# State-space stage of a two-block model: decay rows repeated across partitions by DMA in place of products of ones

## What is computed

```python
xbc = silu(causal_conv4(xbc))            # xs: 16 heads of 64; bm, cm: 4 groups of 128 states
dt = softplus(dt_raw + dt_bias)
a_cum = cumsum(dt * -exp(a_log), within the chunk)
seg = a_cum[:, :, :, None] - a_cum[:, :, None, :]
lmat = exp(where(tril, seg, -inf))       # per head, 0 above the diagonal
cb = einsum('bclgn,bcsgn->bclsg', cm, bm)              # scores, per group
y_diag = einsum('bclsg,bclsgr,bcsgrp->bclgrp', cb, lmat, xdt)
states = einsum('bcsgn,bcsgr,bcsgrp->bcgrpn', bm, exp(a_cum[end] - a_cum), xdt)
y_off = einsum('bclgn,bcgrpn,bclgr->bclgrp', cm, carried_states, exp(a_cum))
g = (y_diag + y_off + d_skip * xs) * silu(z)
g = g * rsqrt(mean(g * g, over the 256 of a group) + eps) * norm_w
```

## Time and profile before

| | |
|---|---|
| median of 3 runs | 1828.46 us (1828.44 to 1828.81) |
| the profiled execution: its time / span of its instructions | 1829.15 us / 1827.4 us |
| mean granted TensorE clock | 0.991 |
| PE busy | 1764.4 us (97%) |
| PE weight loads busy | 1415.2 us (77%) |
| DVE busy | 1002.7 us (55%) |
| ACT busy | 574.9 us (31%) |
| POOL busy | 714.4 us (39%) |
| chain that ended last, by engine | PE 75%, DVE 20%, ACT 2% |

### The profile page before, as it was taken

One profiled execution on the slowest core, in us unless ns is written; L12 is line 12 of the kernel. 1 busy time (PEld: TensorE's weight loads), 2 busy tenths in 40 slices (PEclk: granted clock), 3 DMA queues, 4 the chain that ended last, 5 costly groups with the idle time before them and its releaser, 6 DMA issues.

```text
span 1827.4 us, 22151 instructions
## 1 busy us (share of the span) xinstructions
PE 1764.4 (97%) x7938; PEld 1415.2 (77%) x7938; DVE 1002.7 (55%) x1382; ACT 574.9 (31%) x796; POOL 714.4 (39%) x303
## 2 busy tenths in 40 slices
PE   7999999999999999999899999999989999999996
PEld 6877778788888887888778777777748777778885
DVE  4344333333322645113678989897599766576326
ACT  5322222322222224123632333333362323251211
POOL 3433333343444444443344324343314333325445
PEclk9999999999999999999899999999999999999998
DMA  5322222222333323332433222232212222217422
GB/s 200 114 81 81 81 82 92 81 81 81 99 103 92 97 95 131 116 126 69 163 93 114 69 70 93 62 88 81 69 36 92 81 69 69 80 58 252 126 83 92
DMA packets 50091, 175.55 MB, mean 96 GB/s; under 512 B 5217, under 2 KB 5473, under 8 KB 48865
## 3 DMA queue, kind: packets, MB, share of 16 engines
q1 hardware_dynamic: 41472, 152.13, 26.8%
q10 hardware_dynamic: 8544, 22.37, 3.4%
HBM read 166.09 MB, written 8.39 MB: 95 GB/s over the span
## 4 chain that ended last, share of the span: by engine, by line
PE 75%; DVE 20%; ACT 2%; issue 2%; POOL 1%; DMA 0%; ACTq 0%; DVEq 0%; SPq 0%; POOLq 0%
PE bank L330 73%; DVE gate L1065 3%; DVE feats L1053 2%; DVE bias L1053 2%; DVE bias L1553 1%; PE bank L334 1%; DVE top L1549 1%; DVE probs L1053 1%; DVE gT L1415 1%; DVE gate L1097 1%; DVE nmax L1092 1%; DVE tmp L1053 1%; DVE probs L1104 1%; DVE wide L1408 1%; POOL w_lo L308 1%
## 5 line engine op out<-in xcount | busy, mean ns | idle before, releaser
L308 POOL TENSOR_TENSOR w_lo<-raw,w_hi 128x1024 fp32r<-128x1024 f32 x280 | 688.8, 2464 | 1096.7 <-ACT w_hi L718 1096.7
L330 PE MATMUL bank<-planes_hi,w_hi 128*128 128x512 f32 (+1 forms) x1792 | 709.7, 396 | 19.0 <-DVE w_lo L1128 9.4
L330 PE MATMUL bank<-planes_lo,w_hi 128*128 128x512 f32 (+1 forms) x1792 | 694.8, 388 | 0.0
L330 PE MATMUL bank<-planes_hi,w_lo 128*128 128x512 f32 (+1 forms) x1776 | 687.7, 387 | 0.0
L718 ACT ACTIVATE w_hi<-raw 128x1024 fp32r<-128x1024 f32 x280 | 296.9, 1060 | 909.6 <-PE bank L330 893.3
L330 PEld LDWEIGHTS bank<-planes_hi,w_hi 128*128 128x128 f32 x1792 | 339.7, 190 | 110.2 <-issue 36.6
L330 PEld LDWEIGHTS bank<-planes_lo,w_hi 128*128 128x128 f32 x1792 | 340.1, 190 | 70.2 <-issue 4.8
L330 PEld LDWEIGHTS bank<-planes_hi,w_lo 128*128 128x128 f32 x1776 | 336.2, 189 | 68.3
L330 PE MATMUL bank<-w_hi,planes_hi 128*128 128x512 f32 x512 | 199.9, 391 | 4.2 <-DVE planes_lo L1069 4.2
L330 PE MATMUL bank<-w_hi,planes_lo 128*128 128x512 f32 x512 | 199.2, 389 | 0.0
L330 PE MATMUL bank<-w_lo,planes_hi 128*128 128x512 f32 x512 | 199.2, 389 | 0.0
(11 more groups left out here) (252 smaller groups left out, 1376.5 us busy)
## 6 DMA issues: line engine op xcount, KB each, us to landing
raw<-in_stream SPq DMA_DIRECT2D x282, 512.0 KB, 3.6
h_rows<-feats ACTq DMA_DIRECT2D x4, 1024.0 KB, 7.0
feats<-in_x_t SPq DMA_DIRECT2D x3, 1024.0 KB, 10.5
bias<-in_x_rows ACTq DMA_DIRECT2D x2, 1024.0 KB, 6.2
probs<-in_x_rows ACTq DMA_DIRECT2D x2, 1024.0 KB, 8.4
bias<-h_rows ACTq DMA_DIRECT2D x2, 1024.0 KB, 6.7
probs<-h_rows ACTq DMA_DIRECT2D x2, 1024.0 KB, 8.0
out<-feats ACTq DMA_DIRECT2D x6, 256.0 KB, 2.9
```

The source lines that it names most:

```text
L308: nc.gpsimd.tensor_sub(w_lo[:, s, :], raw[:, s, :], w_hi[:, s, :].bitcast(fp32)).then_inc(lo_ready, 1)
L330: return nc.tensor.matmul(o, a, b, start=start, stop=stop)
```

## The change

The rows of `cumT` and of their exponentials (made in the preparation anyway) are stored to a DRAM tensor `decay_dram` of 32 rows. For each head of a group ACT then issues two loads that repeat one row to 128 partitions: the plain row into `LB[r]`, the exponentiated one into `EB[r]`. Both lists now have four buffers (the rope table's, `kT` and a part of `vN` are free there), so the four heads of a group are loaded ahead: seven loads at the round's first tile, behind the rounding and ahead of `ssd_root`, and the eighth at its second tile, since its buffer holds the squares until then. `pick_row` and `ssd_spread` are gone. `segments` waits for a head's two loads and subtracts in place in SBUF, with a minimum against 0 that keeps exp from growing above the diagonal; the triangle is cut once per group, by multiplying the scores in bank B[0] by `upper`, which holds 1 and 0 now. ACT exponentiates L alone. The rope table's load moves behind round 4. The preparation's rows move from `probs` to `bias`. Numbers of semaphore steps follow.

```diff
@@ -193,8 +194,9 @@
         XBC = [probs, feats]
         Z = [[probsT[:, 0, :], probsT[:, 1, :]], [feats[:, 4, :], feats[:, 5, :]]]
-        LB = [tmp[:, :], probsT[:, 2, :]]
-        EB = [probsT[:, 3, :], qT[:, :]]
+        LB = [rope_q[:, 0, :], rope_q[:, 1, :], vN[:, 0, :, :].rearrange("p j n -> p (j n)"), probsT[:, 2, :]]
+        EB = [probsT[:, 3, :], qT[:, :], kT[:, 0, :], kT[:, 1, :]]
+        SQ = [tmp[:, :], probsT[:, 2, :]]
         QI = [probs[:, 0, :], probs[:, 1, :], probs[:, 2, :], probs[:, 3, :], probsT[:, 0, :], probsT[:, 1, :],
               feats[:, 0, :], feats[:, 1, :]]
@@ -294,9 +297,9 @@
             step(nc.gpsimd.memset(causal, 0.0))
             select(causal[:, S - P:S], ALU.is_ge, BIG, 0, [[-1, P]], 1)
-            step(nc.gpsimd.memset(upper[:, :], 0.0))
-
-            select(upper[:, :], ALU.is_ge, -BIG, 0, [[1, P]], -1)
+            step(nc.gpsimd.memset(upper[:, :], 1.0))
+
+            select(upper[:, :], ALU.is_ge, 0.0, 0, [[1, P]], -1)
             step(nc.gpsimd.memset(last_row[:, :], 0.0))
             select(last_row[:, :], ALU.not_equal, 1.0, -(P - 1), [[0, P]], 1)
             step(nc.gpsimd.memset(padded[:, 0:16], 0.0))
@@ -608,14 +611,10 @@
                     last = mm(dst, vT[:, P * c:P * c + P], states[:, c, :])
                 last.then_inc(ssd_mm, 1)
-            def ssd_spread(g, r):
-                pe.wait_ge(ssd_vec, VEC_STEPS * g + (4, 6, 10, 13)[r])
-                mm([M, O][r % 2][:, :], ones[0:SSD_HEADS, :], gT[0:SSD_HEADS, :]).then_inc(ssd_mm, 1)
-
             def ssd_head(g, r):
-                pe.wait_ge(ssd_vec, VEC_STEPS * g + (10, 13, 15, 16)[r])
+                pe.wait_ge(ssd_vec, VEC_STEPS * g + (7, 9, 11, 12)[r])
                 lanes = slice(64 * (r % 2), 64 * (r % 2) + 64)
-                dst, L, E = B[1 + r // 2], LB[r % 2], EB[r % 2]
+                dst, L, E = B[1 + r // 2], LB[r], EB[r]
                 for c in range(QB):
                     chunk = slice(P * c, P * c + P)
                     last = mm(dst[lanes, chunk], xdt[:, c, 64 * r:64 * r + 64], L[:, chunk], True, c == 0)
@@ -625,9 +624,9 @@
             def ssd_squares(g):
-                pe.wait_ge(ssd_vec, VEC_STEPS * g + 17)
-                mm(M[:, :], ones[:, :], LB[0], True, False)
-                mm(M[:, :], ones[:, :], LB[1], False, True).then_inc(ssd_mm, 1)
+                pe.wait_ge(ssd_vec, VEC_STEPS * g + 13)
+                mm(M[:, :], ones[:, :], SQ[0], True, False)
+                mm(M[:, :], ones[:, :], SQ[1], False, True).then_inc(ssd_mm, 1)
@@ -927,10 +921,9 @@
             act.wait_ge(planes_ready, 48)
-            act.dma_start(rope_q[:, :, :], rope_qk).then_inc(rope_q_loaded, 16)
-            R = [probs[0:SSD_HEADS, k, :] for k in range(4)]
+            R = [bias[0:SSD_HEADS, k, :] for k in range(4)]
@@ -938,12 +931,27 @@
             act.wait_ge(prep_turn, 3)
             step(nc.scalar.activation(R[1], R[1], ACT.Exp))
             signal(nc.scalar.activation(R[2], cumT[:, :], ACT.Exp), prep_turn, 4)
+            act.dma_start(decay_dram[0:SSD_HEADS, :], cumT[:, :]).then_inc(decay_kept, 16)
+            act.dma_start(decay_dram[SSD_HEADS:2 * SSD_HEADS, :], R[2]).then_inc(decay_kept, 16)
+
+            def load_decay(g, r, of, dst):
+                row = SSD_HEADS * of + 4 * g + r
+                act.dma_start(dst, decay_dram[row:row + 1, :].to_broadcast([P, S])).then_inc(decay_loaded[r], 16)
             def ssd_tile(it, k):
                 n = 6 * it + k
                 t = tile_at(T_SSD, n)
                 turn_round(t)
+                if it and k == 0:
+                    if it == 1:
+                        act.wait_ge(decay_kept, 32)
+                    for r in range(4):
+                        if r < 3:
+                            load_decay(it - 1, r, 0, LB[r])
+                        load_decay(it - 1, r, 1, EB[r])
+                if it and k == 1:
+                    load_decay(it - 1, 3, 0, LB[3])
                 if k == 0 and it >= 2:
                     ssd_root(it - 2)
                 if it == GROUPS:
@@ -969,15 +977,13 @@
                 signal(nc.scalar.activation(gate[:, :], src, ACT.Exp, scale=-1.0), silu_exp, n + 1)
             def ssd_exps(g, r):
-                act.wait_ge(ssd_vec, VEC_STEPS * g + (7, 9, 12, 14)[r])
-                n = EXP_STEPS * g + 2 * r + 1
-                signal(nc.scalar.activation(LB[r % 2], LB[r % 2], ACT.Exp), ssd_exp, n)
-                signal(nc.scalar.activation(EB[r % 2], [M, O][r % 2][:, :], ACT.Exp), ssd_exp, n + 1)
+                act.wait_ge(ssd_vec, VEC_STEPS * g + (5, 6, 8, 10)[r])
+                signal(nc.scalar.activation(LB[r], LB[r], ACT.Exp), ssd_exp, EXP_STEPS * g + r + 1)
             def ssd_root(g):
-                act.wait_ge(ssd_mm, MM_STEPS * g + 14)
-                n = EXP_STEPS * g + 9
+                act.wait_ge(ssd_mm, MM_STEPS * g + 10)
+                n = EXP_STEPS * g + 5
                 signal(nc.scalar.activation(gT[:, :], M[:, :], ACT.Ln, bias=EPS, scale=1.0 / 256), ssd_exp, n)
                 signal(nc.scalar.activation(gT[:, :], gT[:, :], ACT.Exp, scale=-0.5), ssd_exp, n + 1)
@@ -1002,6 +1008,7 @@
                         ssd_exps(it - 1, k - 1)
             t = tile_at(T_IDX, 6)
             turn_round(t)
+            act.dma_start(rope_q[:, :, :], rope_qk).then_inc(rope_q_loaded, 16)
             ssd_root(GROUPS - 1)
             act.wait_ge(feat_done, 16 + 2 * GROUPS)
             take(t, QI[6], T_IDX - SK + 7)
@@ -1411,15 +1418,12 @@
                             else:
                                 step(ins)
-            def pick_row(g, r, value):
-                signal(V.tensor_scalar(gT[0:SSD_HEADS, :], cumT[:, :], ident[0:SSD_HEADS, at(4 * g + r)], None, MULT),
-                       ssd_vec, VEC_STEPS * g + value)
-
             def segments(g, r, value):
+                dve.wait_ge(decay_loaded[r], 32 * (g + 1))
                 for c in range(QB):
-                    chunk = slice(P * c, P * c + P)
-                    ins = stt(LB[r % 2][:, chunk], [M, O][r % 2][:, chunk], cumN[:, c, at(4 * g + r)], upper[:, :], SUB, ADD)
+                    cols = LB[r][:, P * c:P * c + P]
+                    ins = V.tensor_scalar(cols, cols, cumN[:, c, at(4 * g + r)], 0.0, SUB, MIN)
                     if c < QB - 1:
                         step(ins)
                     else:
@@ -1427,8 +1431,8 @@
             def operands(g, r, value):
-                dve.wait_ge(ssd_exp, EXP_STEPS * g + 2 * r + 2)
-                L, E = LB[r % 2], EB[r % 2]
+                dve.wait_ge(ssd_exp, EXP_STEPS * g + r + 1)
+                L, E = LB[r], EB[r]
                 step(V.tensor_mul(L, L, B[0][:, :]))
                 signal(V.tensor_mul(E, E, XBC[g % 2][:, 1, :]), ssd_vec, VEC_STEPS * g + value)
@@ -1475,21 +1479,18 @@
                     ssd_normed(it - 2)
                 if it >= 1:
                     ssd_rows(g)
-                    pick_row(g, 0, 4)
+                    scores = B[0][:, :].rearrange("p (c n) -> p c n", c=QB)
+                    step(V.tensor_mul(scores, scores, upper[:, :].unsqueeze(1).to_broadcast([P, QB, P])))
                 if it == 1:
                     dve.wait_ge(rows_stored, STORED[0])
                 silu_tile(6 * it)
                 if it >= 1:
                     ssd_carry(g)
-                    dve.wait_ge(ssd_mm, MM_STEPS * g + 6)
-                    pick_row(g, 1, 6)
-                    segments(g, 0, 7)
+                    segments(g, 0, 5)
                 silu_tile(6 * it + 1)
                 if it >= 1:
-                    dve.wait_ge(ssd_mm, MM_STEPS * g + 7)
-                    pick_row(g, 2, 8)
-                    segments(g, 1, 9)
-                    operands(g, 0, 10)
+                    segments(g, 1, 6)
+                    operands(g, 0, 7)
                 if it == 1:
                     dve.wait_ge(rope_i_loaded, 16)
@@ -1499,16 +1500,13 @@
                 if it == 0:
                     take_decay()
                 if it >= 1:
-                    dve.wait_ge(ssd_mm, MM_STEPS * g + 9)
-                    pick_row(g, 3, 11)
-                    segments(g, 2, 12)
-                    operands(g, 1, 13)
+                    segments(g, 2, 8)
+                    operands(g, 1, 9)
                 silu_tile(6 * it + 3)
                 if it >= 1:
-                    dve.wait_ge(ssd_mm, MM_STEPS * g + 11)
-                    segments(g, 3, 14)
-                    operands(g, 2, 15)
-                    operands(g, 3, 16)
+                    segments(g, 3, 10)
+                    operands(g, 2, 11)
+                    operands(g, 3, 12)
                 silu_tile(6 * it + 4)
             ssd_gated(GROUPS - 1)
             silu_tile(6 * GROUPS + 5)
```

27 lines of the change are left out of this document (12 added, 15 removed).

## The result

| | kernel before | changed kernel |
|---|---|---|
| median of 18 runs, us | 1828.58 (1827.24 to 1830.00) | 1832.78 (1831.28 to 1835.56) |
| profiled execution, us | 1829.15 | 1831.28 |
| its span, us | 1827.4 | 1829.5 |
| granted clock, mean | 0.991 | 0.988 |

The ratio is 1.0025, with a 95% interval of 1.0018 to 1.0031: the changed kernel is slower by 4.2 us in the median. The forecast was 1825.2 us, so the sign was wrong.

A forecast was written before the change was run, and what follows sets the result against it. The prediction took PE and DVE, taking turns, to bound groups 0 to 2, and PE alone group 3. Its terms, -12.15 + 9.75 - 4.2 + 0.9 + 2.4 = -3.3 us, took the median from 1828.46 to 1825.2 us, range 1818 to 1833.

The forecast's parts named there:

- Where DVE and PE meet: Groups 0 to 2, heads to squares: earlier operands bring heads 2 and 3 and the squares about 4.05 us earlier, -12.15 us.
- Rival 5: State-space groups: DVE held by POOL more often or elsewhere, 4.05 us a group shrinks to 1.7: 1832.3 us, chance 0.09.
- The issues: ACT ahead of roots 0, 1 and 2: seven load issues take 3.9 us, each root 3.25 us later, +9.75 us.
- Rival 4: ACT ahead of the roots: issues back up at 1.28 us each, 1840.5 us, chance 0.12.
- The clock: PE behind the longer root stalls: granted clock drops, 0.35 us passes in groups 1 and 2, all in group 3, +2.4 us.
- forecast's own spread: Whole kernel: 1822.8 us if the clock holds to 1827.5 if the stall's cost passes fully in groups 1 and 2.
- Group 3: Last group, where PE is the bound throughout: removing its four products of ones saves 4.2 us.
- The stores: After the preparation: ACT issues two stores ahead of roundings that POOL and then PE wait for, +0.9 us.
- The clock held alone (2): PE around the root stall: matrix work keeps the clock up, 1822.8 us, counted within the forecast's chance.
- DVE not held (3): Groups 0 to 2: new subtractions start whenever DVE reaches them and PE sets the cycle, 1821.6 us, chance 0.10.
- cheap issues (1): ACT ahead of the roots: seven issues take 2.7 us and the clock holds, 1819.3 us, chance 0.15.
- late loads (6): Segment 0: decay loads land late, holding DVE about 8 us in each of three groups, 1849 us, chance 0.03.

The follow-up runs named there:

- e2: Changed kernel with head 3's product of C and decay ahead of head 2's two products: 1828.56 us.
- e3: Changed kernel with both edits, e1's loads behind the root and e2's earlier head 3 product: 1817.08 us.
- e8: e1's kernel with ACT's rounding of a group's last tile, which starts POOL's subtractions, held until DVE has done head 3's two products: 1815.60 us.
- e1: Changed kernel with the seven broadcast-load issues of a group behind the root's two activations instead of ahead of them: 1819.79 us.
- b1: Kernel before, with both stores and seven unread broadcast loads a group added ahead of each root: 1839.09 us.
- e5: Changed kernel with three unread products of ones on PE ahead of the wait for the root in groups 1 to 3: 1830.11 us.
- c0: Changed kernel unedited, run and profiled again: 1832.86 us.
- e6: Changed kernel with five load issues ahead of the root carrying the bytes of seven, two pairs of rows merged: 1824.82 us.
- e4: e1's kernel with four unread products of ones a group put back on PE where the spreads stood: 1823.58 us.
- f2: e7's kernel with head 2's products first again, plus four unread products of ones a group on PE: 1822.62 us, against 1808.80 without those products.
- e7: e3's kernel with the segments' subtractions done by ACT instead of DVE: 1811.26 us.

## Why the prediction was wrong

**The step that failed** is the one under "Where DVE and PE meet": "Heads 2 and 3, the tile behind them and the squares come ... about 4.05 us, earlier". Its first half is nearly exact. Relative to the root, head 2's operands were ready 2.20 us earlier (forecast 2.23) and head 2 began 4.00 us earlier (4.05). The mask took 0.70 us, the unheld segment 1.25 (1.26), the held ones 3.27. But I carried the 4.05 us to the squares without costing head 3. ACT's saved exponential of E, 0.63 us, which I used for the middle steps, brings POOL forward in the last step too: POOL comes 1.37 us earlier, DVE's last product only 0.73 us, and the 0.33 us by which that product had escaped turn into a hold. PE then reaches the squares 2.17 us later after head 2, per group: 6.5 us where the sum had 0. Rival 5 named the mechanism (POOL's delay falls elsewhere), with 1.7 us left per group, against a measured 4.00 - 2.17 = 1.83, at a chance of 0.09; that its 1832.3 us lies so near the median is in part luck, since the profile's own terms come to +1.5 us. e2, e3 and e8 show the cause: 4.2 us came back in e2, 1.48 us a group in e3, and in e8, where the hold alone was removed, 1.9 us a group, nearly all of the 2.17.

**The issues** were mis-sized, not misjudged: 3.25 us a root in the sum, 3.75, 3.71 and 3.32 in the trace, 10.8 against 9.75 us. The ordinary ones are cheaper than taken (0.45 and a gap of 0.03 against 0.5575), but the sixth took up to 0.65 us and the last 1.39, 1.35 and 0.97. e1 confirms the whole: moving them gives 13.0 us, where my two terms for issues and clock make 12.15. b1 gives 10.5 us from the other side. Rival 4 (issues at 1.28 us each) came true for one in seven, at two of three roots.

**The clock** was forecast at 2.4 us. The drop came as said, behind all three stalls, but cost 1.35 us, all in group 3 (e5); in groups 1 and 2, 0 instead of 0.35 each. That holds while DVE, and not PE, sets the group: in b1 the group behind root 0 grew by 1.6 us more than the issues account for. The upper end of the forecast's own spread was added up wrongly too: 1825.2 + 2 x 1.35 is 1827.9, not 1827.5 us.

**Group 3** gave 90.82 - 86.19 = 4.63 us without the clock, 4.2 forecast: 1.16 instead of 1.05 us for each spread.

**The stores** were to cost 0.9 us; the group's start came 0.5 us earlier instead. The removed issue of the rope table, which I put at nothing, is the other edit there; the two weren't tried apart. Nor is the 0.5 us clear of chance: the first load went out at 983.30 us in this profile, and at 982.60 in c0 and 984.09 in e5, with the same instructions up to there. So the 0.9 us of the sum shows in no run.

In the trace the sum is 5.29 (the three roots' delays 1.94, 1.88 and 1.47, without the start's -0.46) - 0.5 - 4.63 + 1.35 = +1.5 us by 1328 us, where mine was -3.3. Of the 4.8 us between them head 3 makes 6.5, the issues 1.0 and the first half of the meeting 0.2 (3.98, 4.00 and 3.99 for 4.05 us); clock, stores and group 3 take back 2.9.

**Rivals.** The clock held alone (2) is ruled out by products 0.43 us apart behind the roots; DVE not held (3) by the subtractions of 3.27 us; cheap issues (1) by the 4.35 us, though e1 shows that the 1819.3 us of that rival is about what the kernel takes once no root waits behind them; late loads (6): no wait of DVE for a decay load was seen. The median's distance of 4.2 us against the profile's 2.1 is not explained; the lower mean clock goes with it, and c0 names one stretch where such a loss occurs in other profiles.

## What to carry to other kernels

When a step is made shorter, follow the engine that shares its port or its triggers as well: here a saved activation moved POOL's start by 0.6 us, and an escape by 0.33 us turned into a hold of 1.9 us on the critical product. Put DMA issues behind the instruction that a bottleneck waits for, and merge them: here they were paid by number on the engine that issued them (e6). Before counting a removed instruction as a gain, ask which engine sets that stretch: the same 16 products were worth 3.8 us while VectorE set it, and about 13 us once it did not.

## What the runs showed that was not expected

- Broadcast loads of 128x512 issued by ACT took 0.33 us for the first and 0.45 us for the next; the last of seven took 1.39, 1.35 and 0.97 us in the changed kernel (and the last two together 1.79 to 2.31 us in e1), but not in b1 (0.45 us) nor with five issues (e6). Why is open. The Trainium skill's page "DMA: Bandwidth & Descriptors", section "Issuing engines are not separate DMA queues", calls an issue's sequencer time usually small relative to the DMA. The trace agrees on the ratio (0.45 us against a median of 5.1 us from issue to landing), and yet seven of them at each of three roots were worth 13 us, since PE stood behind them.
- A wait of 1.60 us in PE's timeline went with 2.17 us more from head 2 to the squares. Recorded lengths of products overlap, so idle time looks short; how much of the other 0.57 us that is was not worked out. Read the price from start to start.
- The clock fell behind stalls of 3.6 to 4.0 us, with products 0.43 us apart, and was held at 1.00 by unread products (e5). The length of the stall alone doesn't decide it: of three stalls of 1.93 us in e6 it fell behind one (0.68 from 1151 to 1154 us) and stayed at 1.00 behind the others, and in b1 it fell behind two of 2.89 us and not behind one of 2.93 us.
- A product of ones with 512 columns and 128 rows took 0.86 us of PE's time in group 3 (e4, f2), the spread with 16 rows 1.05 us. Why the smaller one costs more is open.
- ACT did the four 128-column rectified differences of a segment in 1.71 us (e7), where DVE's four took 3.27 us beside POOL and 1.25 us alone.
